# A decoder trunk kernel in which the up projections of both feed-forward layers are computed as seven block products for eight

## The reference, cut to what matters

```
def conv_ffn(h, w_up, conv_w, conv_b, w_down):   # w_up 1024 x 5632, w_down 2816 x 1024
    u = causal_dwconv(h @ w_up, conv_w, conv_b)  # width 3, over tokens
    g, val = jnp.split(u, 2, axis=-1)
    return (jax.nn.silu(g) * val) @ w_down
h = h + conv_ffn(rms_norm(h, f_norm_g[layer]), f_w_up[layer], ...)
```

## Time and profile before

| what | us |
|---|---|
| median of three runs | 2510.66 |
| the profiled execution, whole | 2509.79 |
| its span, first to last instruction | 2507.8 |
| TensorE busy | 2407.5 |
| VectorE busy | 1389.8 |
| GpSimd busy | 893.9 |
| ScalarE busy | 588.7 |
| feed-forward loop of layer 0 | about 574 to 1250 |
| feed-forward loop of layer 1 | about 1789 to 2465 |

### The profile page before, as it was taken

One profiled execution on the slowest core, in us unless ns is written; L12 is line 12 of the kernel. 1 busy time (PEld: TensorE's weight loads), 2 busy tenths in 40 slices (PEclk: granted clock), 3 DMA queues, 4 the chain that ended last, 5 costly groups with the idle time before them and its releaser, 6 DMA issues.

```text
span 2507.8 us, 29435 instructions
## 1 busy us (share of the span) xinstructions
PE 2407.5 (96%) x10747; PEld 1925.4 (77%) x10747; DVE 1389.8 (55%) x1718; ACT 588.7 (23%) x1035; POOL 893.9 (36%) x380
## 2 busy tenths in 40 slices
PE   6898998999999999999999999989999999999997
PEld 5684666778888888888778778868788888888886
DVE  6855555257555565555671115564855556556656
ACT  4434454122111111111131114441211111111112
POOL 5730000225444444444423332224344444444441
PEclk9999999999999999999999999999999999999999
DMA  4110000211111111111121110021111111111111
GB/s 165 34 59 9 0 0 1 101 34 51 51 50 42 50 50 42 50 50 49 43 101 51 42 42 26 26 93 53 40 51 42 50 50 47 45 49 43 42 50 68
DMA packets 34557, 121.76 MB, mean 49 GB/s; under 512 B 3841, under 2 KB 3969, under 8 KB 34241
## 3 DMA queue, kind: packets, MB, share of 16 engines
q1 hardware_dynamic: 31328, 105.39, 12.6%
q10 hardware_dynamic: 3168, 15.54, 1.6%
HBM read 112.52 MB, written 8.39 MB: 48 GB/s over the span
## 4 chain that ended last, share of the span: by engine, by line
PE 92%; DVE 5%; ACT 2%; issue 1%; DMA 0%; POOL 0%; ACTq 0%; DVEq 0%
PE ps L479 26%; PE ps L481 25%; PE ps L480 25%; PE ps L905 2%; PE ps L883 2%; PE ps L865 1%; PE ps L1032 1%; PE ps L1036 1%; PE ps L1034 1%; PE ps L893 1%; PE ps L379 1%; PE ps L868 1%; PE ps L1085 1%; PE ps L1092 1%; PE ps L1097 1%
## 5 line engine op out<-in xcount | busy, mean ns | idle before, releaser
L302 POOL TENSOR_TENSOR whi<-stage,cons 128x1024 fp32r<-128x1024 f32 x180 | 366.4, 2035 | 1517.7 <-PE ps L481 1460.5
L479 PE MATMUL ps<-ahi,whi 128*128 128x512 f32 x2112 | 846.2, 401 | 43.6 <-POOL wlo L309 18.8
L481 PE MATMUL ps<-ahi,wlo 128*128 128x512 f32 x2112 | 829.1, 393 | 0.0
L480 PE MATMUL ps<-alo,whi 128*128 128x512 f32 x2112 | 829.1, 393 | 0.0
L309 POOL TENSOR_TENSOR wlo<-stage,whi 128x1024 fp32r<-128x1024 f32 x184 | 491.9, 2674 | 39.1 <-ACT whi L1170 25.0
L479 PEld LDWEIGHTS ps<-ahi,whi 128*128 128x128 f32 x2112 | 401.3, 190 | 133.9 <-issue 48.9
L480 PEld LDWEIGHTS ps<-alo,whi 128*128 128x128 f32 x2112 | 401.4, 190 | 85.1 <-issue 2.2
L481 PEld LDWEIGHTS ps<-ahi,wlo 128*128 128x128 f32 x2112 | 400.7, 190 | 85.0
L676 DVE TENSOR_TENSOR hT<-hT,ps 128x512 f32<-128x512 f32 x352 | 237.7, 686 | 204.2 <-PE ps L481 198.8
L479 PE MATMUL ps<-hid_hi,whi 128*128 128x512 f32 x704 | 278.4, 395 | 6.1 <-issue 5.1
L481 PE MATMUL ps<-hid_hi,wlo 128*128 128x512 f32 x704 | 278.1, 395 | 0.0
(11 more groups left out here) (251 smaller groups left out, 2275.1 us busy)
## 6 DMA issues: line engine op xcount, KB each, us to landing
stage<-in_wt SPq DMA_DIRECT2D x184, 512.0 KB, 3.4
hT<-in_xt SPq DMA_DIRECT2D x16, 256.0 KB, 9.4
hT<-in_xt ACTq DMA_DIRECT2D x8, 512.0 KB, 6.4
spill<-hT ACTq DMA_DIRECT2D x1, 4096.0 KB, 12.7
hT<-spill ACTq DMA_DIRECT2D x8, 512.0 KB, 6.7
out<-hT SPq DMA_DIRECT2D x16, 256.0 KB, 2.0
wqb_s<-in_wqb ACTq DMA_DIRECT2D x1, 1024.0 KB, 4.8
wlru_s<-in_wlru ACTq DMA_DIRECT2D x1, 512.0 KB, 6.4
```

What stands on the lines that cost most here:

```text
L302: nc.gpsimd.tensor_tensor(whi[:, slot, :], stage[:, st, :], one_col.to_broadcast([P, 1024]), ALU.mult).then_inc(w_hi, 1)
L479: nc.tensor.matmul(bank, hi, rhs_k[0][:, tok], start=k_first, stop=False)
L480: nc.tensor.matmul(bank, hi, rhs_k[1][:, tok], start=False, stop=False)
L481: return nc.tensor.matmul(bank, lo, rhs_k[0][:, tok], start=False, stop=k_last)
```

## The change: what it does

The first three f of each layer are computed as before. From f = 3 on (19 of 22) gate and value tile are taken together as a 2x2 matrix of blocks (gate, value by first, second half of the depth), the activations as a 2x2 matrix (halves of the depth by halves of the tokens), and the product is formed in the way of Strassen and Winograd: seven block products of 12 matmuls for eight. That needs

- on GpSimd, for each f, four sums of weight blocks over 128x512 (one in `s3_tmp`, three in place in `stage`) and seven subtractions for the low parts; the high parts of the blocks move to ScalarE. Down tiles are split in four blocks. Blocks stand in a ring of four places of 512 columns (slots 2 and 3 of the old ring). Both landing places of `stage` are needed at once, and both are given back together behind the last block (`pool.sem_inc(w_ready, 2)`).
- on VectorE, once in each layer, 16 sums of activations and 16 subtractions for low parts, all 128x512, during f = 0 to 2 and the first down projection; and for each f five additions of a PSUM bank (`mix`), which with two copies on ScalarE take the place of ScalarE's four copies.

Outside the feed-forward part the rotary angles move from GpSimd to VectorE, into a place where it waited; the head weights are copied earlier and the recurrence's splitting stands ahead of the rotary key; in the last chunk of the mLSTM some gates, high parts and low parts come earlier and two parts of the gate product later; the squares of the two feed-forward norms stand in other places of memory; the gates' semaphores are merged. The core of it:

```diff
+            def up_blocks(L, t, i, q, c):          # GpSimd
+                pool.wait_ge(w_landed[0], t * 8 + 16)
+                pool.wait_ge(w_landed[1], t * 8 + 16)
+                nc.gpsimd.tensor_tensor(s3_tmp[:, :], a11, a21, ALU.subtract).then_inc(sem(L + "b_sum"), 1)
+                pool.wait_ge(sem(L + "b_sum"), i * 4 + 1)
+                nc.gpsimd.tensor_tensor(a21, a21, a22, ALU.add).then_inc(sem(L + "b_sum"), 1)
+                block_rest(L, q, c, a11)
+                pool.wait_ge(sem(L + "b_sum"), i * 4 + 2)
+                pool.wait_ge(sem(L + "b_ready"), q + 1)
+                nc.gpsimd.tensor_tensor(a11, a21, a11, ALU.subtract).then_inc(sem(L + "b_sum"), 1)
+                pool.wait_ge(sem(L + "b_sum"), i * 4 + 3)
+                block_rest(L, q + 1, c + 1, a11)
+                block_rest(L, q + 2, c + 2, s3_tmp[:, :])
+                block_rest(L, q + 3, c + 3, a21)
+                block_rest(L, q + 4, c + 4, a12)
+                block_rest(L, q + 5, c + 5, a22)
+                pool.wait_ge(sem(L + "b_ready"), q + 5)
+                nc.gpsimd.tensor_tensor(a12, a12, a11, ALU.subtract).then_inc(sem(L + "b_sum"), 1)
+                pool.wait_ge(sem(L + "b_sum"), i * 4 + 4)
+                block_rest(L, q + 6, c + 6, a12)
+                pool.wait_ge(sem(L + "b_ready"), q + 7)
+                pool.sem_inc(w_ready, 2)
...
+            def up_blocks(i, q, c, first=False):   # TensorE; product = 12 matmuls behind b_ready
+                pe.wait_ge(ev, i * 2 + 2)
+                product(q, c, 0, "B11", True)
...
+                pe.wait_ge(uv, i * 5 + 1)
+                product(q + 1, c + 1, 1, "T2", True)
...
+                product(q + 6, c + 6, 3, "B22", False)
...
+            def up(f, t, i, q, c, j_before, next_block, silu_before):   # ScalarE
+                snapshot(i, f, q)
+                up_block(t, i, q, c, 4)
+                if silu_before:
+                    silu(f - 1)
+                act.wait_ge(b_used, q + 2)
+                up_block(t, i, q, c, 5)
+                act.wait_ge(b_used, q + 3)
+                up_block(t, i, q, c, 6)
+                hidden(f - 1, j_before)
+                act.wait_ge(b_used, q + 4)
+                next_block(0)
+                first_quarter(q)
+                next_block(1)
+                act.wait_ge(b_used, q + 6)
+                next_block(2)
+                act.wait_ge(b_used, q + 7)
+                next_block(3)
...
+            def up1(g, i, q):                      # VectorE
+                value_conv(g * 2, 0)
+                prod(g * 2, 0)
+                mix(i, q, 0)
+                dve.wait_ge(sem(L + "conv"), g * 4 + 2)
+                mix(i, q, 1)
+                lo(g * 2, 0)
+                for n in (2, 3, 4):
+                    mix(i, q, n)
+            def up2(g, i, q):
+                gate_ready(i - 1)
+                gate_conv(g * 2 + 1)
+                conv_step(g * 2 + 1, 1, 0)
+                mix(i, q, 0)
+                for n in (1, 2):
+                    conv_step(g * 2 + 1, 1, n)
...
+                mix(i, q, 1)
+                prod(g * 2 + 1, 1)
+                mix(i, q, 2)
+                lo(g * 2 + 1, 1)
...
+            for k in range(2):                     # VectorE, start of each layer's feed-forward part
+                sums(k)
+            prod(0, 0)
+            lo(0, 0)
+            for k in range(2):
+                t3_lo(k)
```

More of the change, by code:

```diff
@@ L313, in _ @@
                 rest(r, r + 1)
[L315 to L327, removed]
@@ L336, in _ @@
[L336 to L341, removed]
+            with pool.Fori(1, (T_FFN0 + PLAIN) // RING) as i:
+                for r in range(RING):
+                    split(r, (i * (RING // STAGE) + r // STAGE + 1) * 16, i * RING + r + 1, (i - 1) * RING + r + 1)
@@ new lines, in product @@
+            def product(q, c, bank, rhs, first):
+                pe.wait_ge(b_ready, q + 1)
+                for k, (hi, lo) in enumerate(operand(rhs)):
+                    wk = slice(k * P, (k + 1) * P)
+                    nc.tensor.matmul(ps[:, bank, :], block_hi(c)[:, wk], hi, start=first and k == 0, stop=False,
+                                     skip_group_check=True)
+                    nc.tensor.matmul(ps[:, bank, :], block_hi(c)[:, wk], lo, start=False, stop=False,
+                                     skip_group_check=True)
+                    mm = nc.tensor.matmul(ps[:, bank, :], block_lo(c)[:, wk], hi, start=False, stop=(k == 3),
+                                          skip_group_check=True)
+                mm.then_inc(b_used, 1)
@@ L522, in down @@
+            def down(g, q, c, last=False):
                 if not last:
@@ new lines, in act_mlp @@
+            act.sem_inc(ev, 2)
+            evac(0)
+            silu(0)
+            hidden(0, 0)
+            for k in range(2):
+                t3_hi(k)
+            evac(1)
+            silu(1)
+            hidden(1, 1)
+            t3_hi(2)
+            evac(2)
+            for k in range(4):
+                act.wait_ge(sem("t_sum"), t_base(L) + 4 * k + 3)
+                round_piece(k, 3, rpieces[place(k, 5)][:, :])
+            silu(2)
+            t3_hi(3)
+            for k in range(4):
+                act.wait_ge(sem("t_sum"), t_base(L) + 4 * k + 1)
+                round_piece(k, 4, ahi[:, k, halves[1]])
@@ new lines, in act_mlp @@
+            for k in range(4):
+                act.wait_ge(sem("t_lo"), t_count(L, "t1", k))
+                act.wait_ge(sem("t_sum"), t_base(L) + 4 * k + 4)
+                round_piece(k, 2, rpieces[place(k, 4)][:, :])
+            act.wait_ge(w_used, t0 + PLAIN)
+            for n in range(4):
+                up_block(t0 + PLAIN, 0, 0, 0, n)
+            with act.Fori(0, (FG - 3) // 2) as r:
+                for j in range(2):
+                    pair(r * 2 + (j + 1), r * 12 + (t0 + PLAIN + 6 * j), r * 4 + 2 * j, r * 36 + 18 * j, 18 * j)
@@ L684, in pair @@
[L684 to L701 removed]
+                    conv_step(f, 0, i)
@@ new lines, in dve_mlp @@
+            dve.wait_ge(sem(L + "up_read"), 10)
+            gate_conv(2)
+            dve.wait_ge(sem(L + "up_read"), 12)
+            dve.wait_ge(w_used, t0 + 6)
+            sums(3)
+            for n in range(2 * KT):
+                add(0, n, (sem(L + "down"), n + 1) if n < 2 * KT - 1 else (w_used, t0 + PLAIN))
+                if n < 4:
+                    t2_lo(n)
+                elif n == 4:
+                    t3_lo(3)
+                elif n < 9:
+                    t1_lo(n - 5)
+                elif n < 13:
+                    t4_lo(n - 9)
@@ new lines, in dve_mlp @@
+            with dve.Fori(0, (FG - 3) // 2) as r:
+                ch.enter(r, 16)
+                for j in range(2):
+                    pair(r * 2 + (j + 1), r * 4 + 2 * j, r * 36 + 18 * j)
+            ch.leave((FG - 3) // 2)
+            n = FG - 3
+            pair(n + 1, 2 * n, 18 * n)
+            n, g = FG - 2, FG - 1
+            i, q, f = 2 * n, 18 * n, 2 * FG - 1
+            dve.wait_ge(uv, i * 5 + 5)
+            value_conv(g * 2, 0)
+            prod(g * 2, 0)
+            mix(i, q, 0)
@@ L716, in m_tiles @@
+            for n in range(2 * KT):
+                m, s = n % KT, n // KT
+                add(g, n, (sem(L + "down"), (g - 1) * (2 * KT - 2) + (2 * KT - 1 + n + 1)) if n < 2 * KT - 1
+                    else (b_used, BLOCKS), last=True)
+                if m >= 2:
+                    dve_accumulate(dve, next_norm, m - 1, s)
+                if n == KT + 6:
+                    dve_diagonal(dve, ch, next_norm, 0, diag)
         def m_tiles(pe, t0, count, read, ready):
@@ L1814, in _ @@
                     weights(c + 2)
+                if c == TT - 1:
+                    for m in (6, 7):
+                        gate(m, 0)
+                    for m in range(4):
+                        mix_lo(m, 0)
                 dve.wait_ge(sem("m_sd"), c + 1)
@@ L1822, in _ @@
                 ins.then_inc(sem("m_hn"), 1)
-            for m in range(KT):
+            for m in range(4, KT):
                 mix_lo(m, 0)
```

703 lines of the change are left out of this document (481 added, 222 removed).

## The result

The changed kernel takes 2589.7 us (median of 4, 2587.6 to 2592.5) for 2511.0: ratio 1.0314, 95% interval 1.0299 to 1.033. It is 79 us slower; the forecast was 16 us slower, and 2590 lies above its range.

What follows compares the result with a forecast made beforehand. The feed-forward part was taken as bound by TensorE's number of matmuls. 2509.8 + 7 (pairs) - 2 (single f) + 25 (starts) - 14 (outside) = 2525.8, median 2527 us, 0.6% slower; range 2425 to 2575, 8 times in 10.

Steps and rivals of the forecast that it cites:

- What a block product costs: TensorE in the feed-forward pairs: 12 matmuls taken at 2.74 us, so a pair needs 60.8 us of TensorE.
- D: Rival: block products run at the down projection's pitch, 0.06 us more each, +16 us, 2543 us; chance 0.04.
- GpSimd over 512 columns: GpSimd's sums and subtractions: 1.15 us an instruction in turns, 1.25 alone, bounds 1.1 and 1.4.
- B: Rival: GpSimd is the bound at 1.35 us and more an instruction, 2555 to 2572 us; chance 0.09.
- Strict turns: VectorE's convolutions, products and subtractions alternate with all GpSimd instructions on one shared resource; additions from PSUM don't.
- The waits of the first f's course: First f of a pair: `w_ready` after 12.5 us, tiles landed at 17.4, TensorE waits 2.1 to 2.6, then 1.2 to 1.8.
- The second f runs the same course: Second f of a pair: `w_ready` some 12 us after its start, down blocks 1.6 us late; waits 5.5 us a pair.
- C, the clock: Rival: waits at the second f's start drop the clock, costing 2.2 us a pair, 2567 us; chance 0.05.
- The single f at each layer's end: -1 each: Last f of each layer: 2.6 us saved on TensorE, 1.6 us of waits, so -2 us for both layers.
- The starts, +25: Start of each feed-forward part: waits for ScalarE's copy and first blocks, plus half clock, 12.6 us a layer.
- Outside, -14: Edits outside the feed-forward parts: angles -7, head weights and kh -2, last chunk -5 us.
- A, the cover holds: Rival: turns cost nothing and loads come in time, waits 0.5 us a pair, 2437 us; 0.37 including cases towards the forecast.

Runs made afterwards that it cites:

- e8: Changed kernel with the second and third convolution steps in the pairs cut to 16 columns, only time counting: 2502.5 us, ratio 0.9961.
- e2: Changed kernel with filler matmuls, whose result nothing reads, where TensorE would wait: 2585.5 us, ratio 1.0301.
- e6: Kernel of e4 with three edits at a layer's end, among them GpSimd starting the next layer's tiles only once the last hidden values are split: 2461.7 us.
- e4: Changed kernel with each block-part tile loaded in two halves, each sent for once GpSimd has last read its predecessor: 2462.7 us, ratio 0.9801.
- e1: Kernel before the change with only the edits outside the feed-forward parts: 2499.1 us, ratio 0.9949.
- e9: Kernel of e4 with all four half loads of a pair of tiles issued only after block 6: 2566.1 us, ratio 1.0217.

## Why the prediction was wrong

- *What a block product costs* (2.74 us): right, 12 x 0.230 = 2.76. D was not needed. 14 products and a down projection are 61.0 us, for 60.8.
- *GpSimd over 512 columns* (1.25 us alone, 1.15 in turns, bounds 1.1 to 1.4): 1.26 to 1.31 alone, 2.1 to 2.3 with a VectorE step between. B is wrong: GpSimd is busy 41 us of 68. The estimate from the Trainium skill (GPSIMD Engine Reference, section 3.1), 1.35, was too high by 0.04 to 0.09.
- *Strict turns*: right, and e8 shows their price. The Trainium skill (SBUF — State Buffer, Who interferes with whom) has the shared port pair as an exclusive lock, held for a whole instruction, with additions from PSUM outside it; the trace agrees, 2.08 us for a step of 1.28.
- *The waits of the first f's course*: right to half a microsecond in each link (12.5 and 12.75; 5.0 and 5.16; wait 2.1 to 2.6 and 2.38); ahead of the second f's second product 0.9 us for 1.2 to 1.8.
- *"The second f runs the same course"*: this step failed. It has seven long VectorE instructions where the first has four, its last low part comes 16.6 us after its first product and not 12, and the down projection waits 3.0 us for 1.6. The waits of the pair from 984.25 are 6.3 us for 5.5. It has 0.2 to 0.3 us more for the matmuls' pitch, and 0.8 us at the three waits that the sum had at nothing: the last matmul ahead of each is alone for its whole 0.39 us, and the first behind it starts 0.33 us ahead of the next. So it is 68.0 us and not 66.3: 31 us over 18 pairs. The other 7 us are net: the six pairs with a fall of the clock in the down projection are longer than that, and some others are shorter.
- *C, the clock*: falls came in 13 of the 18 pairs, though in six of them at the down projection and not only at the second f, and cost 1.4 us a pair in the matmuls for 2.2. By its own arithmetic it would have given 2567. e2 shows that it was not worth its price here.
- *"The single f at each layer's end: -1 each"*: this step failed too, +12.3 and +5.3. The forecast counted the matmuls saved and did not follow the last f's hidden values. Before, the gate tile was whole before the value tile began, so its convolution ran beside matmuls. With block products all four quadrants are final only in the last four of seven products, and six convolution steps stand behind them. In layer 0 they take turns with the next layer's tiles: 6.5 us (e6). The late load adds 3.4 us to each (e4). The rest, about 2 us a layer, no run takes away; that it is the length of that chain is argued, not shown.
- *The starts, +25*: right (+27.7), for the reason given; 8.58 us of wait for 6.5 to 7, since the product too met GpSimd's next tile, 3.36 us for 1.2. Behind it half clock cost 1.8 and 2.0 us for 2.2.
- *Outside, -14*: right, -11.8; e1 measured -12.
- *A, the cover holds*: the break-even named, `w_ready` 10.9 us behind P0, was about right. e8 has it at 11.1 and a pair of 62.6 us, 1.6 above the matmuls alone; e4 meets the deadline otherwise, by sending for the tiles before `w_ready`, and gets 61.8 (A had 61.3).
- The range was too narrow at its upper end because one f was followed and the other copied, and the end of a layer stood in the sum as matmuls alone.

## What to carry to other kernels

When work moves from the bound engine to helpers, compare the deadline (here seven products, 19.3 us) with the whole chain of one turn: last use of a buffer, issue, landing, sums, rounding. Averages of busy time did not show it here: VectorE and GpSimd were busy for 43 and 41 us in a pair of 68 us, and for 42 and 40 us in one of 62. The largest single gain here was to give back each part of a buffer at its own last use: this turned 3% slower into 2% faster. Follow every iteration that differs, the second of a pair, the first and the last, by itself.

## What was not expected of the hardware

Half clock need not cost what the records add up to: in the pairs 25 us of it went when the gaps were filled (e2), and the time fell by 3 to 4 us. And a load of half the size landed in 2.6 us (median, 256 KB, e4) for 3.5 (512 KB), though where four were sent at once (e9) the median was 3.5 again.
